# Rotary halves exchanged by transfers within SBUF instead of permutation products, in a two-block transformer kernel

## The reference, cut to what matters

```python
def apply_rope(x, ang):
    half = x.shape[-1] // 2
    ...
    x1, x2 = xf[..., :half], xf[..., half:]
    return jnp.concatenate([x1 * cos - x2 * sin, x2 * cos + x1 * sin], axis=-1).astype(x.dtype)

def apply_axial_rope(x, row, col):
    half = x.shape[-1] // 2
    xr = apply_rope(x[..., :half], rope_angles(row, half))
    xc = apply_rope(x[..., half:], rope_angles(col, half))
    return jnp.concatenate([xr, xc], axis=-1)
```

## Time and profile before

| | us |
|---|---|
| median of 3 runs (1764.02 to 1767.79) | 1765.11 |
| the profiled execution | 1767.74 |
| its span, first to last instruction | 1765.9 |
| PE busy | 1740.2 |
| DVE busy | 1197.1 |
| ACT busy | 817.3 |
| POOL busy | 237.9 |

### The profile page before, as it was taken

One profiled execution on the slowest core, in us unless ns is written; L12 is line 12 of the kernel. 1 busy time (PEld: TensorE's weight loads), 2 busy tenths in 40 slices (PEclk: granted clock), 3 DMA queues, 4 the chain that ended last, 5 costly groups with the idle time before them and its releaser, 6 DMA issues.

```text
span 1765.9 us, 37205 instructions
## 1 busy us (share of the span) xinstructions
PE 1740.2 (99%) x14096; PEld 1671.5 (95%) x14096; DVE 1197.1 (68%) x2082; ACT 817.3 (46%) x1308; POOL 237.9 (13%) x259
## 2 busy tenths in 40 slices
PE   8999999999999999999999999999999999999997
PEld 8998999999999998888999999999998888999997
DVE  7567756767665576666886655766567676887754
ACT  4555544444444333554554443444433445555443
POOL 1030000011000203212330002000111321340001
PEclk9999999999999999999999999999999999999999
DMA  7435555555555543342455555555554343555554
GB/s 266 130 108 177 189 180 184 186 180 184 173 177 169 178 156 129 111 132 96 162 180 171 177 171 175 175 170 168 182 175 136 105 158 105 167 176 183 188 180 132
DMA packets 84312, 288.80 MB, mean 164 GB/s; under 512 B 9072, under 2 KB 15984, under 8 KB 83952
## 3 DMA queue, kind: packets, MB, share of 16 engines
q1 hardware_dynamic: 79856, 283.14, 48.5%
q10 hardware_dynamic: 4352, 4.20, 0.8%
HBM read 285.96 MB, written 1.34 MB: 163 GB/s over the span
## 4 chain that ended last, share of the span: by engine, by line
PE 90%; DVE 5%; ACT 2%; issue 1%; DMA 0%; POOL 0%; SPq 0%; DVEq 0%; ACTq 0%
PE PS L857 27%; PE PS L859 27%; PE PS L858 27%; DVE w_lo L1512 2%; PE PS L1371 1%; PE PS L1334 1%; ACT w_hi L453 1%; PE PS L1374 1%; ACT S_all L733 1%; PE PS L1342 1%; PE PS L1360 1%; PE PS L1294 0%; PE PS L1352 0%; DMA raw<-stream 0%; PE PS L1051 0%
## 5 line engine op out<-in xcount | busy, mean ns | idle before, releaser
L1512 DVE TENSOR_TENSOR w_lo<-raw,w_hi 128x1024 fp32r<-128x1024 f32 x525 | 669.3, 1275 | 297.7 <-ACT w_hi L453 287.2
L857 PE MATMUL PS<-x_hi,w_hi 128*128 128x272 f32 (+1 forms) x2832 | 821.0, 290 | 3.1 <-DVE w_lo L1512 3.0
L859 PE MATMUL PS<-x_hi,w_lo 128*128 128x272 f32 (+1 forms) x2832 | 810.8, 286 | 0.0
L858 PE MATMUL PS<-x_lo,w_hi 128*128 128x272 f32 (+1 forms) x2832 | 808.8, 286 | 0.0
L453 ACT ACTIVATE w_hi<-raw 128x1024 fp32r<-128x1024 f32 x525 | 551.2, 1055 | 521.7 <-PE PS L859 514.4
L857 PEld LDWEIGHTS PS<-x_hi,w_hi 128*128 128x128 f32 x2832 | 535.8, 189 | 16.2 <-issue 14.0
L859 PEld LDWEIGHTS PS<-x_hi,w_lo 128*128 128x128 f32 x2832 | 536.4, 189 | 0.0
L858 PEld LDWEIGHTS PS<-x_lo,w_hi 128*128 128x128 f32 x2832 | 535.4, 189 | 0.7
L857 PE MATMUL PS<-a_hi,w_hi 128*128 128x272 f32 (+1 forms) x1280 | 364.8, 285 | 1.3 <-DVE a_lo L2142 1.3
L859 PE MATMUL PS<-a_hi,w_lo 128*128 128x272 f32 (+1 forms) x1280 | 363.7, 284 | 0.0
L858 PE MATMUL PS<-a_lo,w_hi 128*128 128x272 f32 (+1 forms) x1280 | 363.0, 284 | 0.0
(11 more groups left out here) (301 smaller groups left out, 1267.8 us busy)
## 6 DMA issues: line engine op xcount, KB each, us to landing
raw<-stream SPq DMA_DIRECT2D x525, 512.0 KB, 3.4
biasB<-rpbz ACTq DMA_DIRECT2D x16, 256.0 KB, 3.1
G<-b1mats SPq DMA_DIRECT2D x2, 1024.0 KB, 7.1
h<-xT SPq DMA_DIRECT2D x4, 272.0 KB, 5.7
out<-qk SPq DMA_DIRECT2D x4, 256.0 KB, 3.0
mat<-mats SPq DMA_DIRECT2D x1, 952.0 KB, 5.3
v_tok<-u_rows SPq DMA_DIRECT2D x4, 142.0 KB, 3.1
mat<-u_rows SPq DMA_DIRECT2D x4, 142.0 KB, 3.9
```

The source lines that it names most:

```text
L857: pe.matmul(ps, hi, rh, start=first, stop=False)
L858: pe.matmul(ps, hi, rl, start=False, stop=False)
L859: return pe.matmul(ps, lo, rh, start=False, stop=last)
L1512: dve.tensor_tensor(w_lo[:, slot, :], raw[:, slot, :], w_hi[:, slot, :].bitcast(F32), ALU.subtract).then_inc(lo_done, 1)
```

## The change

The permutation matrices and the products with them go. In their place ACT issues four transfers for each tile, each of which copies 32 partitions of `qk` to the neighbouring group of 32 partitions of a tile of `G` (32 x 272 floats, 34 KB). DVE waits until all four have landed, multiplies the tile of `G` by the sine table in place, and POOL goes on as before. Each of the ten rotated tiles has its own tile of `G`, G10 to G19. The gates that are written to G10 and on wait until POOL has added the last of them.

An exchange of groups of 32 partitions fits branch A. In branch C the partners are 16 apart, so the host permutes the channels of each head of C (`AXIAL`: 0-15, 32-47, 16-31, 48-63) in the weights of qC and kC, in their gains and in the tables. Scores don't change when query and key are permuted alike.

The transfers of kA are issued at t = 1, those of qA 0 to 3 at t = 17 to 20, and all twenty of branch C at t = 21, each after ACT's split of that t. DVE multiplies at t = 4, 18 to 21 and 22 respectively, after its split and eviction of that t.

```diff
+SWAP_AT = {1: [0], 17: [1], 18: [2], 19: [3], 20: [4], 21: [5, 6, 7, 8, 9]}
+ROPE_AT = {4: [0], 18: [1], 19: [2], 20: [3], 21: [4], 22: [5, 6, 7, 8, 9]}
...
+                def swap(k):
+
+                    if k < 5:
+                        act.wait_ge(out_free, ob + (o + (0 if k == 0 else 15 + k) + 1))
+                    else:
+                        act.wait_ge(aux_free, l * LAYER_A + (B1_AUX + CASTC_IN_LAYER + k - 5 + 1))
+                    for g in range(4):
+                        act.dma_start(swap_tile(k)[32 * g:32 * g + 32, :], qk[32 * (g ^ 1):32 * (g ^ 1) + 32, ROPE_TILES[k], :])\
+                           .then_inc(swapped[k], 16)
+
...
+                    for k in SWAP_AT.get(t, []):
+                        swap(k)
...
-                        if what in ("swapA", "swapC"):
-                            if what == "swapA":
-                                tt = 0 if i == R_KA else 16 + i - R_QA
-                                pe.wait_ge(out_free, ob + (o + tt + 1))
-                            else:
-
-                                pe.wait_ge(aux_free, l * LAYER_A + (castC_at + C_TILES.index(i) + 1))
-                            perm = mat[:, M_PA:M_PA + P] if what == "swapA" else mat[:, M_PC:M_PC + P]
-                            mm = pe.matmul(PS[:, b, 0:L], perm, qk[:, i, :], start=True, stop=True)
...
+                def rope(k):
+
+                    dve.wait_ge(swapped[k], (l + 1) * 4 * 16)
+                    tab = M_TAB + (L if k < 5 else 3 * L)
+                    dve.tensor_tensor(swap_tile(k), swap_tile(k), mat[:, tab:tab + L], ALU.mult).then_inc(swap_scaled, 1)
+
...
-                            dve.tensor_tensor(G[:, 17 + swaps % 3, :], PS[:, b, 0:L], mat[:, tab + L:tab + 2 * L], ALU.mult)\
-                               .then_inc(aux_free, ax.up())
...
+                    for k in ROPE_AT.get(t, []):
+                        rope(k)
...
+                    if j == 10:
+                        dve.wait_ge(roped, l * ROPES + ROPES)
...
-                    pool.wait_ge(aux_free, l * LAYER_A + (B1_AUX + 1 + k + 1))
+                    pool.wait_ge(swap_scaled, l * ROPES + k + 1)
                     step(pool.tensor_tensor(qk[:, i, :], qk[:, i, :], mat[:, tab:tab + L], ALU.mult))
-                    pool.tensor_tensor(qk[:, i, :], qk[:, i, :], G[:, 17 + n % 3, :], ALU.add).then_inc(roped, 1)
+                    pool.tensor_tensor(qk[:, i, :], qk[:, i, :], swap_tile(k), ALU.add).then_inc(roped, 1)
```

More of the change, by code:

```diff
@@ L30 @@
 LAM_INIT = 0.2
+AXIAL = np.r_[0:16, 32:48, 16:32, 48:64]
 BLK = 8
@@ L58 @@
 C_TILES = [R_KC] + [R_QC + t for t in range(4)]
-QKV_EVENTS = {0: [("stat", 0)], 4: [("swapA", R_KA)], 16: [("sumC", 0)]}
+ROPE_TILES = [R_KA] + [R_QA + t for t in range(4)] + C_TILES
+ROPES = len(ROPE_TILES)
+SWAP_AT = {1: [0], 17: [1], 18: [2], 19: [3], 20: [4], 21: [5, 6, 7, 8, 9]}
+ROPE_AT = {4: [0], 18: [1], 19: [2], 20: [3], 21: [4], 22: [5, 6, 7, 8, 9]}
+QKV_EVENTS = {0: [("stat", 0)], 16: [("sumC", 0)]}
 for _t in range(6):
     QKV_EVENTS[7 + _t] = [("v", _t)]
[L62 to L65, removed]
+QKV_EVENTS[20] = [("castC", i) for i in range(5)]
 QKV_EVENT_LIST = [e for t in range(QKV_T) for e in QKV_EVENTS.get(t, [])]
@@ L116 @@
 NC = C_RW + KD * 20
-M_ID, M_ONES, M_PA, M_PC = 0, P, 2 * P, 3 * P
-M_SEL16 = 4 * P
+M_ID, M_ONES = 0, P
+M_SEL16 = 2 * P
 M_SEL4 = M_SEL16 + 9 * 17
@@ L234, in router_cols, with swap_tile @@
             return S_f[:, 1664 + at:1664 + at + n]
+        def swap_tile(k):
+            return G[:, 10 + k, :]
         gates_bc = Gf[:, 0:16 * SEQ].rearrange("p (e t) -> p e t", e=16)
@@ L250, in build @@
         c_squared, c_rstd, roped = sem("c_squared"), sem("c_rstd"), sem("roped")
+        swapped, swap_scaled = [sem(f"swapped{k}") for k in range(ROPES)], sem("swap_scaled")
         scores_out, logits_ready, exp_done, rden_ready = (
@@ L1285, in _ @@
                         b = aux_begin()
[L1286 to L1295 removed]
+                        if what == "v":
                             pe.wait_ge(out_free, ob + (o + 6 + i + 1))
@@ L1995, in _ @@
                         b = aux_bank()
[L1996 to L2001, removed]
-                            dve.tensor_tensor(G[:, 17 + swaps % 3, :], PS[:, b, 0:L], mat[:, tab + L:tab + 2 * L], ALU.mult)\
-                               .then_inc(aux_free, ax.up())
-                            swaps += 1
-                        elif what == "v":
+                        if what == "v":
                             step(dve.tensor_copy(v_tok[:, 0:2, i * P:(i + 1) * P],
@@ L2257, in _ @@
                 sum_squares(ob + FFN_UP)
-                SWAPS = [(k, e) for k, e in enumerate(QKV_EVENT_LIST) if e[0] in ("swapA", "swapC")]
-                for n, (k, (what, i)) in enumerate(SWAPS):
-                    tab = M_TAB + (0 if what == "swapA" else 2 * L)
-                    pool.wait_ge(aux_free, l * LAYER_A + (B1_AUX + 1 + k + 1))
+                for k, i in enumerate(ROPE_TILES):
+                    tab = M_TAB + (0 if k < 5 else 2 * L)
+                    pool.wait_ge(swap_scaled, l * ROPES + k + 1)
                     step(pool.tensor_tensor(qk[:, i, :], qk[:, i, :], mat[:, tab:tab + L], ALU.mult))
-                    pool.tensor_tensor(qk[:, i, :], qk[:, i, :], G[:, 17 + n % 3, :], ALU.add).then_inc(roped, 1)
+                    pool.tensor_tensor(qk[:, i, :], qk[:, i, :], swap_tile(k), ALU.add).then_inc(roped, 1)
                 for s in range(PAIRS):
@@ L2335, in constants @@
     (cr, sr), (cc, sc) = table(32, row), table(32, column)
-    for k, a in enumerate((cosA, sinA, np.concatenate([cr, cc]), np.concatenate([sr, sc]))):
+    for k, a in enumerate((cosA, sinA, np.concatenate([cr, cc])[AXIAL], np.concatenate([sr, sc])[AXIAL])):
         c[:, M_TAB + k * L:M_TAB + (k + 1) * L] = np.concatenate([a, a])
@@ L2427 @@
         qa, ka, va, qb, kb, vb, qc, kc, vc, gates = np.split(w, np.cumsum([512, 128, 128, 512, 512, 512, 512, 128, 128]), axis=1)
+        kc, qc = (x.reshape(D, -1, HD)[:, :, AXIAL].reshape(D, -1) for x in (kc, qc))
         for part in (ka, kc, kb, va, vc, vb, qc[:, pairs], qa[:, pairs], qb, gates):
@@ L2450 @@
     for l in range(LAYERS):
-        col[:, C_QN + 2 * l] = np.tile(a["qnorm_c_2"][l], 2)
-        col[:, C_QN + 2 * l + 1] = np.tile(a["knorm_c_2"][l], 2)
+        col[:, C_QN + 2 * l] = np.tile(a["qnorm_c_2"][l][AXIAL], 2)
+        col[:, C_QN + 2 * l + 1] = np.tile(a["knorm_c_2"][l][AXIAL], 2)
         col[:, C_SINK + 9 * l:C_SINK + 9 * l + 8] = a["sink_a_2"][l][None, :]
```

8 lines of the change are left out of this document (2 added, 6 removed).

## The result

The changed kernel takes 1781.97 us (median of 4 runs, 1779.96 to 1783.19), the kernel before beside it 1764.68 (4 runs). The ratio is 1.0091, 95% interval 1.0078 to 1.0103: 0.9% slower. The forecast was 1767.1, the range ended at 1776. The change is slower by more than even the dearest issue of the forecast would have made it.

The account below looks back on a forecast made before the run. PE was taken as the bound (busy 99%), its saving turning into a wait. Later logits, 1.3 us in layer 0 and 0.3 in layer 1, plus 0.4 for t = 1, made 1765.11 + 2.0 = 1767.1; range 1757.5 to 1776.

Parts of the forecast that it names:

- the price of an issue: ACT's time to issue one transfer of 32 partitions: taken as 0.52 us, with bounds 0.33 and 0.73.
- the start of the burst: When ACT's twenty branch C issues begin at t = 21: 689.0 in layer 0, 1369.5 in layer 1.
- the tail: From the last issue to the first logits, through splits, evictions and five sine products on DVE: 6.6 us.
- what follows the first logits: Everything after DVE starts the first logits was to shift one for one with that moment, adding nothing.
- rival B: ACT's issues on the path to the first logits cost 0.61 to 0.73 us: 1771.1 to 1776.3 us, chance 0.28.
- 0.2 a layer at t = 1: Four issues at t = 1 delay chunk 5's split; net cost 0.2 us a layer after PE's saving at t = 4.
- Landing is covered: Before the last sine product, splits and eviction cover a transfer's landing up to 4.5 us, so it costs nothing.
- POOL at nothing: POOL's ten branch C instructions start later, near 702 instead of 699, but cost nothing; 1 us late, layer 1 pays some.
- ahead of gates 0 and 1: Where PE, waiting for DVE's evictions, was to lose its saving: some 3 to 5 us in each layer.
- A (cheap issues): Issues are cheap and logits start when PE's scores are done: 10.0 us gained, 1755.1 (1758.7 at 0.33 an issue), chance 0.25.
- C (landing): Transfers sharing engines with the weight stream land later than 4.5 us; at 6 us, 1.5 more a layer, 1770.1, chance 0.05.
- 10.0 us, the most that the change can bring: PE's saving: 9.2 us from twenty products gone in both layers and 0.8 us of waits for the evicted tile.

Follow-up runs that it names:

- run 6: Changed kernel with branch C by products and branch A's transfers left out (A's halves not exchanged): 1761.12 us, ratio 0.9973 to the kernel before.
- run 2: Changed kernel with one transfer of 128 partitions per tile instead of four of 32 (halves not exchanged), 20 issues in all: 1760.51 us, ratio 0.9972.
- run 5: Changed kernel with branch A by transfers, but branch C by permutation products as in the kernel before: 1768.3 us, ratio 1.0014.
- Run 4: Changed kernel with eight idle products on PE in layer 0, ahead of its wait for the meta queries' logits: 1782.12 us, ratio 1.0091.
- runs 10 and 11: Changed kernel with A by products, C by transfers in the attention steps, twenty or eight issues a layer: 1762.02 us (0.9973) and 1761.21 us (0.9972).
- run 1: Changed kernel without any of its eighty transfers, sine products reading their own tile (halves not exchanged): 1759.16 us, ratio 0.9964.
- run 11: Changed kernel with A by products and C by transfers in attention steps 0 and 1, eight issues a layer: 1761.21 us, ratio 0.9972.

## Why the prediction was wrong

The mechanism was the one forecast: the products go, and a burst on ACT at t = 21 holds up the split of chunk 25, DVE's row behind it, and the first logits. Its likeliest case failed by size, in four terms of the sum: the price of an issue (5.8 us too low in both layers together), the start of the burst (3.7), the tail (2.8) and what follows the first logits (2.9, put at nothing). The range gave room to the price alone. With the 0.66 of the burst in its own sum it would have said 1773; the rest lies in three terms that had no range. The differences below are against the kernel before at the same mark.

- **"Start of the burst 689.0 and 1369.5."** Measured against the first mark, it started at 688.76 + 2.16 = 690.9 and 1379.37 - 8.09 = 1371.3: 1.9 and 1.8 us late. The forecast set the issues at t = 18 to 20 against PE's saving and let the saving win. Here the reasoning failed most, not only a size: run 6 prices A's transfers at 7.2 us where C goes by products. I had looked at the splits that they hold up, and not at the landing, which I worked out for C alone; for qA DVE waits 1.6 us in layer 0, for one that takes 4.95, and 1.0 in layer 1.
- **"The price of an issue, 0.52."** 0.66 in the burst: 13.3 - 10.4 = 2.9 us a layer. It fell in rival B (0.61 to 0.73). 0.51 is what the first issue of a row takes; the others take 0.61 and more. The row by engine was right, the row by shape wrong, and run 2 shows why: partitions and bytes don't enter.
- **"Tail 6.6 us."** 710.03 - 702.03 = 8.0: 1.4 more. The five products were put at 2.1 and took 3.35, the split behind them 1.78 instead of 1.17. The forecast named the cause (both inputs in SBUF, POOL at work) and allowed 0.2 for it. In the kernel of run 5, where C's products bring the operand through PSUM, five of them took 2.28, beside POOL too; and one with both inputs in SBUF while POOL idled (680.97, after) took 0.42. That agrees with the Trainium skill ("SBUF — State Buffer", "Who interferes with whom"): a DVE instruction with two SBUF inputs contends with a GpSimd instruction that reads SBUF, and one with at most one SBUF input doesn't, outside the two-port modes.
- Start, price and tail make 1.9 + 2.9 + 1.4 = 6.2 in layer 0 and 6.1 in layer 1. With the 1.3 and 0.3 of the forecast they make 7.5 and 6.4. Measured from the first mark: 710.03 + 2.16 - 704.71 = 7.5, and 1400.64 - 8.09 - 1386.24 = 6.3. The sum closes.
- **"From there on everything follows that moment one for one."** Layer 0 lost 9.9 and not 7.5, layer 1 6.8 and not 6.3. These 2.4 and 0.5 us lie behind the logits. In layer 0 they can be taken apart: 0.4 more from logits to turn (9.1 against 8.7; DVE's split at 714.11 took 2.12 us, before 1.68), and 2.0 from the turn to the scores of pair 1, in which PE doesn't wait and its clock is low (0.50 from 720 to 723). Run 4 shows that these 2.0 are the clock's: with it at 1.00 they are gone. The 0.5 of layer 1 stay open.
- **"0.2 a layer at t = 1."** This held: PE waits 0.66 and 0.5 us for the split behind these issues, and the product that went was worth 0.46. That the kernel after was 2.2 us ahead at the first mark is for the most part other waits that fell otherwise in this execution (the execution before had one of 2.1 for `small`, this one 1.1), 1.2 of it before anything was changed.
- **"Landing is covered"** held for C (no wait for DMA behind the burst) and so did **"POOL at nothing"** in layer 0; in layer 1 POOL made PE wait 1.7 us.
- **Not foreseen:** PE's wait of 3.3 us before the first scores, for the copy of the meta queries that stands in ACT's list behind the burst. It lies inside the slack of the burst, but shows that PE's waits were not only "ahead of gates 0 and 1".

By the Trainium skill ("DMA: Bandwidth & Descriptors", "Issuing engines are not separate DMA queues") the sequencer's time to start a DMA is usually small beside the DMA. Here 0.61 stands beside a median landing of 2.5 us, a quarter of it. Twenty in a row are 13.3 us; they overlap with each other's landings and with what stands ahead of them in ACT's list, and not with what stands behind.

Rivals: A (cheap issues) is refuted by 0.66; B held in its size of the issue, but with its own 1771 to 1776 it would still have been short by the start, the tail and what follows the logits. C (landing) was right about qA, where it wasn't placed, and wrong about C.

Of the "10.0 us, the most that the change can bring", the runs show this much: with C's products out of the way (runs 10 and 11) the kernel gains some 5 us, 1.3 of them clock; with A's gone and nothing in their place (run 6) some 5; with all twenty gone (run 1) 6.4, as DVE's row ahead of the logits then sets the time in layer 0.

## What to carry to other kernels

A DMA's price on the engine that issues it is per issue, so cut their number (whole tiles, neighbouring tiles together) before their bytes, and put them where that engine idles: with C's forty moved a few steps later the kernel took 17 us less. Before trading PE time for anything, ask what stands in the other engine's list behind the new work; taking branch A's products away was worth some 5 us, and the transfers in their place cost 7.2. Where a step is fed by a dependent row of small instructions (here C's norms), a late split or landing behind it reaches PE: of 3.7 us of DVE's waits there PE lost 2.0, and 1.2 more by its clock. And compare two profiles by the distance from a common mark, not by absolute times.

## What the runs showed of the hardware

- An issue on ACT took 0.47 us alone, 0.61 in fours, 0.63 to 0.66 in rows of five and twenty, for 32 as for 128 partitions and for 34 KB as for 136 KB. In a row the first took 0.51 and each further one mostly 0.61.
- Issues started while work ahead of them in ACT's list was still to come: a split at 702.77 began within a pair of issues from 702.08 to 703.37 (run 11).
- From issue to landing, a transfer of 34 KB within SBUF took 1.9 us at least, 2.5 in the median and 5.0 at most; the line of the transfers, after:

```profile
L734 ACTq DMA_DIRECT2D G<-qk x80: 514/612/1192, 623.6 to 1392.0; - x80
DMA to landing us min/median/max: 1.9/2.5/5.0
```

- Five DVE products with both inputs in SBUF took 3.35 us beside POOL, and 2.28 with one input in PSUM beside POOL.
- PE's granted clock fell to 0.50 to 0.56 behind waits of 1.7 to 4.1 us, and stood at 1.00 where idle products filled one of 3.9; 2.0 us of the path hung on that. It fell without any wait too, behind the twenty narrow products for C's roots (layer 1 of the kernel before and of run 6, layer 0 of runs 1 and 6); there 0.50 to 0.57.
